# A second GLU unit ahead of x, B and C, a rearranged first LayerNorm, and another order of the scan

## The reference

```python
h = layer_norm(x, g, b)
u_glu, z, xbc, dt, gate_a, gate_b = split(h @ w_in)
# conformer branch
a, g = split(u_glu);  v = a * sigmoid(g)
v = silu(layer_norm(causal_dwconv(v, 31 taps)));  y_a = v @ w_conv_out
# state space branch: 32 heads of 64, 4 groups, state 128, chunks of 128
xbc = silu(causal_dwconv(xbc, 4 taps));  dt = softplus(dt + bias)
y = ssd_chunked(x, dt, -exp(a_log), B, C) + x * d
y = y * silu(z);  y = y * rsqrt(mean_of_group(y * y) + eps) * norm_w
y_b = y @ w_ssm_out
mix = (sigmoid(gate_a) * y_a + sigmoid(gate_b) * y_b) @ w_o
h = layer_norm(2**0.25 * h + mix);  h = layer_norm(2**0.25 * h + conv_ffn(h))
```

## Time and profile before

| | |
|---|---|
| median of 3 runs | 2266.19 us |
| profiled execution, its own time | 2266.07 us |
| its span | 2264.3 us, granted clock 0.993 |
| TensorE busy | 2192.8 us, 97% |
| VectorE busy | 1464.1 us, 65% |
| ScalarE busy | 963.0 us, 43% |
| GpSimd busy | 44.7 us, 2% |

### The profile page before, as it was taken

One profiled execution on the slowest core, in us unless ns is written; L12 is line 12 of the kernel. 1 busy time (PEld: TensorE's weight loads), 2 busy tenths in 40 slices (PEclk: granted clock), 3 DMA queues, 4 the chain that ended last, 5 costly groups with the idle time before them and its releaser, 6 DMA issues.

```text
span 2264.3 us, 31759 instructions
## 1 busy us (share of the span) xinstructions
PE 2192.8 (97%) x12964; PEld 1922.5 (85%) x12964; DVE 1464.1 (65%) x1859; ACT 963.0 (43%) x1393; POOL 44.7 (2%) x29
## 2 busy tenths in 40 slices
PE   7999999999999999999999999999999999999997
PEld 5888777777887788888999999999998988888886
DVE  5778898899857656645676685235367668722544
ACT  4446666632534444433547443223233565422321
POOL 0000011100000000000200000000000000000000
PEclk9999999999999999999999999999999999999998
DMA  4222333322221322243221212222222112222221
GB/s 160 93 95 90 105 103 110 106 75 93 89 82 72 112 93 93 97 146 130 97 75 38 94 60 93 90 94 94 93 75 97 57 56 94 93 93 93 93 93 56
DMA packets 35695, 208.20 MB, mean 92 GB/s; under 512 B 4930, under 2 KB 6978, under 8 KB 12132
## 3 DMA queue, kind: packets, MB, share of 16 engines
q1 hardware_dynamic: 29280, 194.66, 24.2%
q10 hardware_dynamic: 6276, 11.57, 1.6%
HBM read 204.05 MB, written 2.17 MB: 91 GB/s over the span
## 4 chain that ended last, share of the span: by engine, by line
PE 80%; DVE 10%; DVEq 4%; ACT 3%; issue 1%; ACTq 1%; DMA 0%
PE PS L524 25%; PE PS L526 24%; PE PS L528 24%; DVE vout L2022 3%; DVEq L2015 2%; PE PS L1023 1%; DVE hres L1964 1%; PE PS L611 1%; DVE wlo L1778 1%; DVEq L1963 1%; ACT whi L1132 1%; PE PS L997 1%; DVE zres L1962 1%; PE PS L855 0%; PE PS L1013 0%
## 5 line engine op out<-in xcount | busy, mean ns | idle before, releaser
L524 PE MATMUL PS<-ahi,whi 128*128 128x512 f32 (+2 forms) x2376 | 732.6, 343 | 13.6 <-DVE upad L2455 3.2
L526 PE MATMUL PS<-alo,whi 128*128 128x512 f32 (+2 forms) x2376 | 720.2, 338 | 0.0
L528 PE MATMUL PS<-ahi,wlo 128*128 128x512 f32 (+2 forms) x2376 | 719.5, 338 | 0.0
L1778 DVE TENSOR_TENSOR wlo<-raw,whi 128x2048 fp32r<-128x2048 f32 x174 | 399.4, 2297 | 454.3 <-ACT whi L1132 453.7
L1132 ACT ACTIVATE whi<-raw 128x2048 fp32r<-128x2048 f32 x168 | 321.7, 1915 | 668.3 <-PE PS L528 665.2
L524 PEld LDWEIGHTS PS<-ahi,whi 128*128 128x128 f32 x2376 | 414.1, 189 | 76.6 <-issue 24.9
L528 PEld LDWEIGHTS PS<-ahi,wlo 128*128 128x128 f32 x2376 | 413.2, 188 | 48.1
L526 PEld LDWEIGHTS PS<-alo,whi 128*128 128x128 f32 x2376 | 413.6, 188 | 47.6 <-issue 1.2
L524 PE MATMUL PS<-f2hi,whi 128*128 128x264 f32 (+2 forms) x800 | 214.9, 314 | 0.0
L526 PE MATMUL PS<-f2lo,whi 128*128 128x264 f32 (+2 forms) x800 | 214.8, 314 | 0.0
L528 PE MATMUL PS<-f2hi,wlo 128*128 128x264 f32 (+2 forms) x800 | 214.8, 314 | 0.0
(11 more groups left out here) (317 smaller groups left out, 2648.2 us busy)
## 6 DMA issues: line engine op xcount, KB each, us to landing
raw<-weights SPq DMA_DIRECT2D x181, 1024.0 KB, 4.7
acs_b<-acs_rows ACTq DMA_DIRECT2D x34, 256.0 KB, 3.3
const<-const ACTq DMA_DIRECT2D x2, 1232.0 KB, 5.3
x_in<-x_t SPq DMA_DIRECT2D x4, 512.0 KB, 5.2
out_t<-hres SPq DMA_DIRECT2D x16, 128.0 KB, 1.7
cols<-columns SPq DMA_DIRECT2D x1, 385.0 KB, 6.9
const<-const SPq DMA_DIRECT2D x1, 256.0 KB, 6.7
acs_rows<-acs_rows ACTq DMA_DIRECT2D x1, 64.0 KB
```

Of the source, the lines that this page charges most:

```text
L524: nc.tensor.matmul(o, wh, h, start=first, stop=False)
L526: nc.tensor.matmul(o, wh, h, start=False, stop=False)
L528: mm = nc.tensor.matmul(out[j], wl, hi[j], start=False, stop=last)
L1778: v.tensor_tensor(wlo[s][:, :], raw[s][:, :], whi[s][:, :].bitcast(F32), ALU.subtract).then_inc(lo_ready, 1)
```

## The change

It has three parts. (1) The front: the mean is summed by four matmuls on pair sums; constants are loaded by ScalarE's queue; GpSimd makes the high and low part of half of the first GLU unit, ScalarE the other half and dt's 32 columns a block; dt's matmuls are 32 columns wide; transposes of ident and other fillers stand in the front; the inverse deviation is spread from rows. (2) The scan: masks and taps in another order, both heads of a pair issued in turn, 27 taps of the even tile of each group instead of 31, three buffers for the squares. (3) glu0 has two units, so tile 1 is there before xbc and has two taps behind each xbc unit; z_glu has its last two units used as gate_b's first two, and gate_b has two left. Late tiles are 3 and 5; tiles 2, 4 and 6 end their last four taps, and tile 1 its last nine, in and before ssm_out.

```diff
-TAPS_AT = [0, 4, 4, 9, 10, 14, 15, 19, 20, 20]
+TAPS_AT = [0, 4, 5, 8, 9, 11, 13, 16, 27]
-FIRST_TAPS = 3
+FIRST_TAPS = (3, 2)
+TILE1_TAPS = 22
-    ahead = [("dt", 1, 1, KD), ("glu0", 1, 2, KD), ("xbc", XBCT // 2, 2, KD), ("z_glu", 4 * GROUPS - 1, 2, KD)]
+    ahead = [("dt", 1, 1, KD), ("glu0", 2, 2, KD), ("xbc", XBCT // 2, 2, KD), ("z_glu", 4 * GROUPS, 2, KD)]
-        ysq4 = [at(f"ysq4{s}", ssd0 + b * TB, T) for s, b in enumerate((4, 5, 6, 11))]
+        ysq4 = [at(f"ysq4{s}", ssd0 + b * TB, T) for s, b in enumerate((4, 5, 6))]
...
+            half = slice(0, KD * P)
+            pool.wait_ge(raw_in[1], 16)
+            nc.gpsimd.tensor_copy(whi[1][:, half], raw[1][:, half])
+            nc.gpsimd.drain()
+            nc.gpsimd.tensor_tensor(wlo[1][:, half], raw[1][:, half], whi[1][:, half].bitcast(F32), ALU.subtract
+                                    ).then_inc(glu_lo, 1)
+            pool.wait_ge(hi_ready, 1)
+            nc.gpsimd.tensor_tensor(dt_block(wlo[0]), dt_block(raw[0]), dt_block(whi[0]).bitcast(F32), ALU.subtract
+                                    ).then_inc(lo_ready, 1)
...
-            mean(n_in, xin_ok)
-            variance(n_in)
-            spin(8)
-            spread(n_in)
-            spin(16)
+            for _ in range(20):
+                nc.tensor.matmul(bank(7, P, 384), warm[:, :], warm[:, :], start=True, stop=True)
+            pe.wait_ge(const_in, 16)
+            for j in range(X_PARTS):
+                pe.wait_ge(xin_ok, j + 2)
+                mm = nc.tensor.matmul(bank(4), ones, x_sum[j][:, :], start=j == 0, stop=j == X_PARTS - 1)
+            mm.then_inc(n_in["pe"].sem, 1)
+            for k in range(KD):
+                after(pe, n_in["act"], k + 1)
+                chunk_sums(sq1[k % 2], k == 0, k == KD - 1).then_inc(n_in["pe"].sem, 1)
+                for _ in range(2 if k < KD - 1 else 0):
+                    nc.tensor.transpose(bank(7, P, 384), ident, ident)
+            spin(4, 5)
...
+            spin(7, 3)
+                nc.tensor.matmul(bank(0, parts=HEADS), whi[0][:, w], a, start=k == 0, stop=False)
+                nc.tensor.matmul(bank(0, parts=HEADS), whi[0][:, w], b, start=False, stop=False)
+                return nc.tensor.matmul(bank(0, parts=HEADS), wlo[0][:, w], a, start=False, stop=k == KD - 1)
...
-            linear(WORK["xbc"], ahi, alo, T, hooks={0: dt_turns, 2: a_spread, DT_AT - 1: acs_sums})
+            linear(WORK["xbc"], ahi, alo, T, hooks={0: dt_turns, 3: a_spread, DT_AT - 1: acs_sums})
...
+                def pair(j):
+                    hold(pe, mc_ok, g * GH + 2 * (j + 1), "pe")
                     for c in range(CHUNKS):
+                        for hh in range(2):
+                            q = 2 * j + hh
...
-            linear(WORK["gate_b"], ahi, alo, T, amid={1: group_sums, 2: group_scales}, begun=1)
+            linear(WORK["gate_b"], ahi, alo, T, amid={0: group_sums, 1: group_scales})
...
-                if k >= 4:
-                    act.wait_ge(ysq_sum, k - 3)
+                if k >= 3:
+                    act.wait_ge(ysq_sum, k - 2)
...
+            act.wait_ge(y_mm, HEADS)
+            sigmoids(stage, 4 * GROUPS - 2, gb, 4, 2 - 4 * GROUPS)
+            for k in range(GP, 3 * GP):
+                y_square(k)
+            split_next(stage, 2 * GROUPS - 1, 1)
+            sigmoids(stage, 4 * GROUPS - 1, gb, 4, 2 - 4 * GROUPS)
+            for k in range(3 * GP, XT):
+                y_square(k)
...
-                w = FIRST_TAPS * (2 * i + s - 1)
-                long_taps([0], max(w, 0), min(w + FIRST_TAPS, TAPS))
+                for k, n in enumerate(FIRST_TAPS):
+                    w = n * (2 * i + s - 1)
+                    long_taps([k], max(w, 0), min(w + n, TAPS))
...
-            late_tiles = [u for u in range(2, KD, 2)]
+            late_tiles = [3, 5]
...
+                    for q in range(4):
                         mask(q)
+                    taps(1)
+                    y_out(0)
+                    taps(2)
+                    low_next(stage, 2 * g, 1)
+                    taps(3)
+                    y_out(1)
+                    mask(4)
+                    mask(5)
+                    taps(4)
+                    y_out(2)
+                    taps(5)
+                    mask(6)
+                    low_next(stage, 2 * g + 1, 0)
+                    mask(7)
+                    taps(6)
+                    y_out(3)
+                    taps(7)
...
             mask(0)
             mask(1)
             long_taps([KD - 1], TAPS_AT[1], LAST_TAPS[0])
+            gated_sums(range(0, GP))
             mask(2)
-            gated_sums(range(0, GP))
...
             long_taps(late_tiles, 0, TAPS_GATE)
+            long_taps([1], TILE1_TAPS, TILE1_TAPS + 3)
...
-            for u in (0, 1, 3, 5):
-                add_up(vout[:, u * T:(u + 1) * T], vout_ok)
+            add_up(vout[:, 0:T], vout_ok)
...
+                    u = 2 * i + s
+                    if u < TAPS - TAPS_AT[-1]:
+                        long_taps([2, 4, 6], TAPS_AT[-1] + u, TAPS_AT[-1] + u + 1)
+                    elif u < KD - 1:
+                        w = TILE1_TAPS + 3 + 2 * (u - 4)
+                        long_taps([1], w, w + 2)
+                        add_up(vout[:, 2 * (u - 3) * T:(2 * (u - 3) + 1) * T], vout_ok)
+                    else:
+                        add_up(vout[:, T:2 * T], vout_ok)
```

More of the change, by code:

```diff
@@ L456, in _ @@
                 sp.dma_start(x_in[:, c], xT[:, c]).then_inc(x_in_s[j], 16)
[L457 to L461, removed]
+            sp.dma_start(raw[1][:, :], wstream[SOURCE[1]]).then_inc(raw_in[1], 16)
+            sp.dma_start(raw[0][:, 0:KD * P], wstream[SOURCE[0]][:, 0:KD * P]).then_inc(raw_in[0], 16)
             for u in range(2, WORK["gate_b"].u0 + 1):
@@ new lines, in _, with dt_tile @@
+            spin(4, 5)
+            after(pe, n_in["dve"], KD + 1)
+            for c in range(CHUNKS):
+                r = slice(32 * c, 32 * c + 1)
+                mm = nc.tensor.matmul(bank(4 + c, P), ones[r, :], rstd[r, 0:P], start=True, stop=True)
+            mm.then_inc(n_in["pe"].sem, 1)
+            spin(7, 3)
+            def dt_tile(k):
+                a, b, w = ahi[:, k * T:(k + 1) * T], alo[:, k * T:(k + 1) * T], slice(k * P, k * P + HEADS)
+                nc.tensor.matmul(bank(0, parts=HEADS), whi[0][:, w], a, start=k == 0, stop=False)
+                nc.tensor.matmul(bank(0, parts=HEADS), whi[0][:, w], b, start=False, stop=False)
+                return nc.tensor.matmul(bank(0, parts=HEADS), wlo[0][:, w], a, start=False, stop=k == KD - 1)
@@ L751, in _ @@
+            pe.wait_ge(glu_lo, 1)
+            pe.wait_ge(lo_ready, 1)
             for k in range(KD):
                 after(pe, n_in["lo"], k + 1)
-                for stage in pair:
-                    tile(stage, ahi, alo, T, 1, 0, 0, [k])
+                mm = dt_tile(k)
+                if k == KD - 1:
+                    mm.then_inc(unit_done, 1)
+                tile(WORK["glu0"], ahi, alo, T, 1, 0, 0, [k])
+            pe.wait_ge(lo_ready, 2)
             tile(WORK["glu0"], ahi, alo, T, 1, 0, 1, range(KD))
+            claim(WORK["glu0"], 0, 1)
@@ L758, in dt_turns @@
+            for m in range(2):
+                tile(WORK["glu0"], ahi, alo, T, 1, 1, m, range(KD))
             def dt_turns():
@@ L1429, in _ @@
                                  ).then_inc(ss_std, 1)
-            sigmoids(stage, 0, gb, 4)
-            gate(stage, 1, gb)
             y_high(range(0, 3))
-            gate(stage, 2, gb)
+            gate(stage, 0, gb, 2)
             y_high(range(3, 9))
-            gate(stage, 3, gb)
+            gate(stage, 1, gb, 2)
             y_high(range(9, XT))
@@ L1790, in tap, with layer_norm @@
                 return v.scalar_tensor_tensor(acc[:, sh:n], ps[:, 0:n - sh], w, acc[:, sh:n], ALU.mult, ALU.add)
-            def layer_norm(n, src, hi, lo, each=None, pe_odd=True, units=(), late=None, rows=None):
+            def layer_norm(n, src, hi, lo, each=None, pe_odd=True, units=(), late=None):
                 after(dve, n["pe"], 1)
@@ L2000, in folding @@
                 return each
+            v.memset(warm[:, :], 0.0).then_inc(xin_ok, 1)
             v3 = vpad[:, :].rearrange("p (k t) -> p k t", k=KD)
             v.memset(v3[:, :, 0:TAPS - 1], 0.0)
[L2004 to L2009 removed]
+            for j in range(X_PARTS):
+                dve.wait_ge(x_in_s[j], 16)
+                v.tensor_tensor(x_sum[j][:, :], x_in[:, 2 * j * T:(2 * j + 1) * T], x_in[:, (2 * j + 1) * T:(2 * j + 2) * T],
+                                ALU.add).then_inc(xin_ok, 1)
+            layer_norm(n_in, x_in, ahi, alo)
+            low_at(2, True)
             def long_taps(tiles, a, b, start=None):
```

223 lines of the change are left out of this document (106 added, 117 removed).

## The result

The changed kernel takes 2269.61 us (median of 20 runs, 2268.55 to 2271.48) beside 2266.09 us of the kernel before on the same chip (20 runs, 2263.50 to 2269.74). The ratio is 1.0015, 95% interval 1.0009 to 1.0021: 3.5 us slower, which lies inside the 0.2% called no difference above, though the interval leaves out 1. The forecast was 2268. The profiled execution has a span of 2267.7 us against 2264.3, a granted clock of 0.992 against 0.993.

The account below looks back on a forecast made before the run. TensorE, busy 97% of the span, was taken as the bound, with VectorE nearly full in ssm_out. Terms -5.3 + 3.1 - 10.4 + 15.1 - 1.1 = +1.4 us gave 2267.6, say 2268; range 2253 to 2280.

Parts of the forecast that it names:

- The front: Stretch to the first projection matmul: four pieces taken out, start near 23.8 instead of 30.78, -5.3 us with dt's cost.
- The +1.75: In the front: dt's 32-column matmuls alternating with 128-column ones cost 0.22 us a pair of changes, eight times.
- x, B and C: The xbc stage: VectorE's unit grows to 11.13 us, over TensorE's 10.9, dt's small operations pile up; +3.1, bounds 0 to +6.
- Groups 0 to 2: Scan groups: fewer taps, masks ahead of taps, heads of a pair alternating; -10.4 us, bounds -14 to -5.
- Group 3: Last scan group: ScalarE's fourth square waits for VectorE's first sum, its heads come late; 4.7 us of TensorE stall.
- The rival: VectorE saturates, in its clock part: TensorE's longer stalls halve its clock behind them, 1.7 us lost a dip; chance 0.17.
- gate_b: Behind the scan: last sum 3.6 us late, one tile covers y's normalisation; with group 3, +15.1 of stalls, bounds +6 to +20.
- ssm_out: Last term, up to the conv mean: rounds of two units shorten from 24.05 us to 23.7 or 24.2, then 21.8; -1.1.
- the cold front: Rival at the front: thinner fillers, clock stays at half, the front's gain is gone; 2274, chance 0.14.
- the slow narrow matmuls: Rival at the front: dt's 32-column matmuls cost as much as full fp32 ones; +15 us, 2283, chance 0.05.
- The covers hold: Faster rival: no ScalarE wait (4.7), xbc absorbed (3.1), one low part in time; 2258, chance 0.28.
- VectorE saturates: Slower rival, xbc to the mean: VectorE regains less of its 33 us idle, stalls halve TensorE's clock; +6, 2274, chance 0.17.

Follow-up runs that it names:

- the first run: The kernel before with the front's edits and nothing else: 2259.20 us, ratio 0.9962.
- the second set: The runs in which the kernel before, unchanged, took 2265.16 us (28 runs), beside the kernels from tile 1's taps left out to the gate units early.

## Why the forecast was right, and where its terms were off

The balance held: a gain ahead of the scan and in it, a loss behind it, and next to nothing left. The sum was off by 2 us while its terms were off by up to 3.3, in both directions: front and groups gained 4.6 us more than forecast, and the other three stages lost 6.6 more. So the balance was understood, but that the total came out this near is in part luck.

- **The front** was right in its pieces: -7 and a start near 23.8, measured 24.07. The +1.75 for 32- and 128-column matmuls in turn is the term that was wrong: they cost nothing that shows, 1.38 us for six, and six wide ones 0.227 to 0.233 apart are 1.36 to 1.40. The row from which it was taken, a tile behind head matmuls of 64 columns, still shows the 0.1 us: the tile's second matmul follows its first (295.11) after 0.335 us, and the others after 0.23. The Trainium skill, TensorEngine Tiling (Array Packing), Tiling Modes, says that changing the tiling mode drains TensorE; between these two shapes no row here shows such a cost.
- **x, B and C**: the mechanism, VectorE over TensorE's 10.9 us a unit with dt's small operations on top, was right, as the run without 21 of the taps shows. Its size was +4.6, inside the bounds but 1.5 over. That run shows also that more than half of the 2.3 us by which TensorE waits for xdt hangs on the same taps (0.9 are left).
- **Groups 0 to 2**: the term was too small twice. A pair takes 1.02 us, not 1.18, from the first matmul to the next tile (16 starts, 54.7 ns apart on average); and pair 3's stall is 0.67, not 1.5. That the pair's order gives nothing by itself was in no step of the sum: its four times 0.33 us a group were counted as a gain of their own, and the run with that part alone shows waits in their place. Groups 0 to 2 gain once masks and taps stand in the new order too (6.8 us, with all 31 taps), and again as much in the changed kernel, which has four taps fewer a group.
- **Group 3**: right as a mechanism and nearly so in size; 4.7 us forecast, 5.1 measured, and the own buffer gives 5.2 us back in time. What the term left out is the clock, which the forecast had only as a rival: it fell to 0.50 (1.2 GHz of 2.4) for 6.8 us in and behind each of three waits of 4.5 to 5.1 us. In group 3 pair 1 took 1.90 us for 1.02 and the tile behind it 7.05 for 5.59, 2.3 us together. The rival had priced such a fall at 1.7 us, from the two of 3.4 us between xbc and the mean; the front's was 6.8 us even before.
- **gate_b**: 3.6 us forecast for the last sum, 4.5 measured; y's start forecast 86.8 us after the group's zero, measured 90.4, with two of the three falls of the clock ahead of it; 20.1 us from y's start to ssm_out's second unit forecast, 19.4 measured (457.41 to 476.83). The forecast put this down to lost cover, one tile behind the scales where three had stood. The kernel without the moved unit confirms it: there the same late order waits 1.0 us for the last sum and 1.6 before ssm_out's second unit. But lost cover is only one half: with the squares first, and with the gate units and two low parts early, 6.4 us come back under the same small cover.
- **ssm_out**: -1.1 forecast, +1.1 measured. The rounds came as forecast: from low part to low part 23.7 (503.92 to 527.63) and 24.0 us (527.63 to 551.62). The start did not. ssm_out's third unit got its low part 14.5 us after the second unit began, 12.5 before; the clock is at half until 481.17, 4.3 us in which half as much is done, and that is these 2.0. The kernel with the fourth buffer agrees: 3.1 us at half clock behind the second unit's start, and the low part after 13.9.

Of the rivals, the cold front and the slow narrow matmuls fell with the first run. *The covers hold* named the right three places. Its 2258 is what the kernel with the last squares first and the gates early reaches, by other means: not because the waits were absent, but because two of them were an order of ScalarE's and one a buffer. *VectorE saturates* has part of the truth, in xbc and in the halved clock. Its 33 us of idle VectorE are those of the xbc and ssm_out windows alone; the whole stretch from 58.29 to 574.59 has 62.7 (516.30 less 453.64).

By cause, the 3.5 us are: front -7.3; scan order -0.9, within the noise; the buffer taken away +5.2; the moved unit with its taps +6.5. The last is a remainder between runs and has both signs in it: a gain in the groups, the loss of 4.4 in xbc, and the waits behind the scan. With all the repairs of the late part the kernel with the moved unit is 7.0 us below the kernel before; the kernels without it are 8.2 and 8.3 below, and the front alone 7.3. These four are not told apart by the times, so nothing here shows that moving the unit, or the new scan order, gains anything in the end. What stays open is the wait of 2.8 us that is left before the column sums, and whether tile 1's taps could stand anywhere without a cost; neither was tried.

## What to carry to other kernels

A unit of work that is moved ahead takes its cover with it. Before moving one, list the chain that it hid, here sums, root, reciprocal, scales, normalisation and low parts, and order the helpers' queues for the shorter cover in the same edit: last inputs of the chain first, weight splits and gates in its gaps. When one buffer is dropped, look for what queues behind the engine that must wait for it: here a square that nobody needed soon held back two heads that TensorE needed at once. And a wait of 5 us can cost more than its length, when the clock falls behind it. Last, time each part of a change alone: here the front's gain of 7.3 us was hidden under the losses of the other two.

## What the runs showed of the hardware

fp32r matmuls of 32 and of 128 columns follow each other at 0.23 us in the front with no gap. Sixteen 64-column matmuls on alternating halves of the columns started two by two, 6 ns apart, a new two every 109 ns (54.7 ns a matmul), where matmuls of the same 128 positions over all columns start 109 ns apart, and so do those of one head alone: the two halves work side by side. The Trainium skill, TensorEngine Tiling (Array Packing), Tiling Modes, has tiles working independently; the trace agrees: 16 in turn are shown with 1.09 us, as 8 of one head alone were the earlier trace rows. The length of the clock's fall was not expected and is not settled. The changed kernel has 6.8 us at half clock at each of its waits of 4.5 to 5.1 us. At the same wait of 5.3 us the kernel with the fourth buffer has 3.4 us and the one with the taps moved 6.8. The kernel with the heads in turn has 6.8 at a wait of 2.8, and the kernel before has 3.4 where no wait is longer than 1.9 (from 551.9). An estimate of the price of one fall is therefore 1.7 to 3.4 us, with no row that tells beforehand which. The falls also go with the spread between executions of one kernel: of the 28 runs of the kernel before in the second set, the 14 that took 2263.7 to 2264.7 us had a mean granted clock of 0.994 or 0.995, and the 6 that took 2267.9 to 2269.5 had 0.992; the changed kernel had 0.991 or 0.992 in all its 20.
